# Expert stage: five row gathers ahead, units 0 and 1 interleaved, GpSimd drains at other places, a split norm vector and last product

## What is computed

```python
h2 = rmsnorm_2(x, norm2_g[l])
x = x + hier_moe(h2, ...)          # 32 experts of width 256, each token goes to 2 experts of one group
return rmsnorm_2(x, norm_f_g)

def expert_block(args):            # one block of rows, one expert
    xb, e = args
    return (jax.nn.silu(xb @ w_gate[e]) * (xb @ w_up[e])) @ w_down[e]
```

## Time and profile before

| | us |
|---|---|
| median of 3 runs | 1306.07 |
| the profiled execution, its time | 1303.1 |
| its span | 1301.1 |
| expert stage in the span | about 1056 to 1301 |
| TensorE busy | 1255.3 (96%) |
| VectorE / ScalarE / GpSimd busy | 640.0 / 522.9 / 568.9 |

### The profile page before, as it was taken

The page is one execution under the profiler, slowest core; times in us unless marked ns, Lnnn a source line. Parts: engine busy times, 40 slices in busy tenths (PEclk is TensorE's granted clock), DMA queues, the critical chain, the costliest instruction groups (busy, mean ns, idle before and its releaser), DMA issues.

```text
span 1301.1 us, 18979 instructions
## 1 busy us (share of the span) xinstructions
PE 1255.3 (96%) x6642; PEld 960.5 (74%) x6642; DVE 640.0 (49%) x1248; ACT 522.9 (40%) x884; POOL 568.9 (44%) x715
## 2 busy tenths in 40 slices
PE   7999999999999999999999999999999989998896
PEld 6767777787888888888888788777888865554462
DVE  4868768725542422222225765757243276342443
ACT  5657544435444324133144534145322300543444
POOL 4633323334655655555545664424644212341321
PEclk9999999999999999999999999999999999998899
DMA  6422222112334333333333333322427999999996
GB/s 219 109 65 55 67 58 65 50 49 81 98 96 113 115 97 97 115 97 113 97 98 97 97 96 83 82 49 70 126 81 265 359 331 386 417 417 416 417 417 246
DMA packets 223104, 208.38 MB, mean 160 GB/s; under 512 B 36034, under 2 KB 197556, under 8 KB 218804
## 3 DMA queue, kind: packets, MB, share of 16 engines
q1 hardware_dynamic: 209728, 191.87, 44.7%
q0 software_dynamic: 9504, 13.66, 2.8%
q10 hardware_dynamic: 3796, 1.86, 0.5%
HBM read 209.43 MB, written 20.45 MB: 177 GB/s over the span
## 4 chain that ended last, share of the span: by engine, by line
issue 40%; POOL 31%; PE 19%; DMA 4%; DVE 3%; SPq 2%; POOLq 1%; ACT 0%; DVEq 0%; ACTq 0%
POOL wlo L670 31%; PE bank L2408 4%; PE bank L2036 3%; PE bank L2038 3%; PE bank L2037 3%; PE bank L2425 3%; SPq L543 1%; DMA gu<-in_w_exp_up 1%; DMA xe<-part_rows,tabi 1%; PE side L2066 1%; DMA part_rows<-xe,tabi 1%; DMA xe<-x_rows,tabi 1%; PE side L2038 1%; PE side L2037 1%; PE side L2036 1%
## 5 line engine op out<-in xcount | busy, mean ns | idle before, releaser
L670 POOL TENSOR_TENSOR wlo<-raw,whi 128x256 fp32r<-128x256 f32 x644 | 497.6, 804 | 525.9 <-ACT whi L838 525.7
L2037 PE MATMUL bank<-actB_lo,whi 128*128 128x512 f32 x608 | 236.7, 389 | 0.0
L838 ACT ACTIVATE whi<-raw 128x1024 fp32r<-128x1024 f32 x161 | 169.0, 1051 | 152.6 <-PE bank L2038 125.0
L2036 PE MATMUL bank<-actB_hi,whi 128*128 128x512 f32 x576 | 227.8, 395 | 0.5 <-POOL wlo L670 0.5
L2038 PE MATMUL bank<-actB_hi,wlo 128*128 128x512 f32 x576 | 224.4, 390 | 0.0
L2036 PE MATMUL bank<-actA_hi,whi 128*128 128x512 f32 x400 | 157.0, 392 | 1.7 <-DVE actA_lo L1269 1.6
L2038 PE MATMUL bank<-actA_hi,wlo 128*128 128x512 f32 x400 | 155.7, 389 | 0.0
L2037 PE MATMUL bank<-actA_lo,whi 128*128 128x512 f32 x400 | 155.7, 389 | 0.0
L2408 PE MATMUL bank<-gu,xeT 128*64 128x256 f32 x1088 | 128.4, 386 | 8.5 <-issue 5.9
L2037 PEld LDWEIGHTS bank<-actB_lo,whi 128*128 128x128 f32 x608 | 114.2, 188 | 24.0 <-issue 1.0
L2036 PEld LDWEIGHTS bank<-actB_hi,whi 128*128 128x128 f32 x576 | 108.2, 188 | 25.9 <-issue 2.3
(11 more groups left out here) (448 smaller groups left out, 1703.3 us busy)
## 6 DMA issues: line engine op xcount, KB each, us to landing
gu<-in_w_exp_gate SPq DMA_DIRECT2D x64, 512.0 KB, 15.4
gu<-in_w_exp_up SPq DMA_DIRECT2D x64, 512.0 KB, 16.3
dn<-in_w_exp_down SPq DMA_DIRECT2D x30, 1024.0 KB, 17.8
raw<-in_w_in SPq DMA_DIRECT2D x57, 512.0 KB, 3.8
raw<-in_w_up SPq DMA_DIRECT2D x32, 512.0 KB, 3.9
raw<-in_w_down SPq DMA_DIRECT2D x32, 512.0 KB, 3.7
raw<-in_w_out SPq DMA_DIRECT2D x16, 512.0 KB, 3.8
raw<-in_w_in SPq DMA_DIRECT2D x16, 256.0 KB, 3.2
```

The costliest lines, as they stand in the source:

```text
L670: ins = nc.gpsimd.tensor_tensor(wlo[:, slot, at], raw[:, slot, at], whi[:, slot, at].bitcast(F32), ALU.subtract)
L838: a(whi[:, c % RING, :], raw[:, c % RING, :], ACT.Copy).then_inc(hi_made, 1)
L2036: mm(b[:, :], w_hi, hi[:, k, :], start=first, stop=False)
L2037: mm(b[:, :], w_hi, lo[:, k, :], start=False, stop=False)
```

## The change

- **Five gathers at once.** `buffer_of` now gives units 4 and 5 the buffers 5 and 4. Buffer 5 (`xe_far`) lies where `gfin` was, so POOL issues the gather of unit 4 with the first four. The waits for the scatters of units 0 and 1 ahead of gathers 4 and 5 are gone, and so is the wait for `over_ready` ahead of gather 6. Gather 5 waits for `over_listed`.
- **Norm vector in two pieces.** `gfin[0]` is loaded where `gfin` was. `gfin[1]` is loaded by SP after downs 8 and 9, behind a new wait for `over_ready`, because its place is used by a temporary until then. `finish` makes its product in two halves.
- **Loads of unit 4.** SP starts the quarters of unit 4 before it waits for the downs of unit 0.
- **Order of units 0 and 1 on TensorE.** Gates and ups of unit 0, rows of 1, gates and ups of unit 1, turn hidden 0, rows of 2, downs of 0, then iteration 1. The overflow table comes after the downs of unit 1. VectorE copies the rows of unit 1 ahead of `hidden(0)`, makes `hidden(1)` ahead of `y_of(0)`, and runs `list_overflow` after `y_of(1)`.
- **Drains.** The one ahead of scatter 13 is gone. There is now one ahead of `scattered(q)` and `parts_of_unit(q + 1)` for q = 7 and q = 8.
- **Last product shared.** In `finish_last` VectorE multiplies both halves by the gains while the norm is being worked out. Then VectorE scales the first half and ScalarE the second.
- The overflow loop counts its steps with two semaphores instead of five. It isn't entered with these inputs.

```diff
-    return q if q < X_FIRST else (0, 1, 4, 5, 2, 3)[(q - X_FIRST) % X_BUFS]
+    return q if q < X_FIRST else (5, 4, 0, 1, 2, 3)[(q - X_FIRST) % X_BUFS]
...
-            sp.dma_start(gfin[:, :], A["norm_f_g_2"].partition_broadcast(P)).then_inc(S("small_in"), 16)
+            sp.dma_start(gfin[0][:, :], A["norm_f_g_2"][0:L].partition_broadcast(P)).then_inc(S("small_in"), 16)
...
             for q in range(PIECED_E.start, EXTRA_AT + 1):
+                if q in PIECED_E:
+                    gate_up_in_quarters(q)
                 for n in places_of(q):
                     if n >= D_BUFS:
                         sp.wait_ge(S("down_done"), unit_of(n - D_BUFS) + 1)
                         down(n)
+                if q == PIECED_E.stop - 1:
+                    sp.wait_ge(S("over_ready"), 1)
+                    sp.dma_start(gfin[1][:, :], A["norm_f_g_2"][L:].partition_broadcast(P)).then_inc(S("small_in"), 16)
                 if q in PIECED_E:
-                    gate_up_in_quarters(q)
                     continue
...
-            for q in range(X_FIRST):
-                gather(q, tabi[:, 1, q:q + 1], S(f"gathered{q}"))
+            for q in range(X_FIRST + 1):
+                gather(buffer_of(q), tabi[:, 1, q:q + 1], S(f"gathered{q}"))
...
-                if q in (LAST_E - 3, LAST_E - 1):
+                if q == LAST_E - 1:
                     pool.drain()
                 pool.wait_ge(S("y_made"), q + 1)
                 scatter(buffer_of(q), tabi[:, 0, q:q + 1], S(f"scattered{q % 2}"))
                 n = q + X_FIRST
-                if n < UNITS_E:
-                    if q < 2:
-                        scattered(q)
-                    if q == 2:
+                if X_FIRST < n < UNITS_E:
+                    if q == 1:
                         pool.wait_ge(S("over_listed"), 1)
-                        pool.wait_ge(S("over_ready"), 1)
...
                 if q + 1 in MIXED_E:
+                    pool.drain()
                     scattered(q)
                     parts_of_unit(q + 1)
...
+            act.wait_ge(S("last_norm_made"), 1)
+            second = x_in(buffer_of(LAST_E))[:, L:]
+            a(second, second, ACT.Copy, scale=gw[:, 13, LAST_E % NT:LAST_E % NT + 1]).then_inc(S("last_squared"), 1)
...
+            def finish_last():
+
+                one_ = slice(LAST_E % NT, LAST_E % NT + 1)
+                first, second = (x_in(buffer_of(LAST_E))[:, n * L:(n + 1) * L] for n in range(2))
+                for n, x in enumerate((first, second)):
+                    dve.wait_ge(S("last_squared"), n + 1)
+                    chain(v.tensor_tensor(x, x, gfin[n][:, :], ALU.mult))
+                dve.wait_ge(S("guess_made"), guesses[0] + 1)
+                chain(v.tensor_tensor(gw[:, 12, one_], gw[:, 10, one_], gw[:, 11, one_], ALU.add))
+                refine(gw[:, 12, one_], gw[:, 13, one_], D, gw[:, 14, one_], gw[:, 15, one_], made=S("last_norm_made"))
+                chain(v.tensor_scalar(first, first, gw[:, 13, one_], None, ALU.mult), S("rows_finished"))
...
-            for q in range(LAST_E):
-                hidden(q % 2, slotv[:, 0, q:q + 1], q + 1)
-                if q == 0:
-                    rows_turned(1, 2)
-                    late_columns()
-                    overflow_columns()
-                    y_of(0)
-                    rows_turned(0, 3)
-                    place_overflow()
-                    continue
+            rows_turned(1, 2)
+            hidden(0, slotv[:, 0, 0:1], 1)
+            late_columns()
+            overflow_columns()
+            hidden(1, slotv[:, 0, 1:2], 2)
+            rows_turned(0, 3)
+            y_of(0)
+            place_overflow()
...
+            gate_up_of(0)
+            turn_rows_of(1)
+            first_gates_of(1, 0)
+            first_gates_of(1, 1)
+            gate_up_of(1)
+            turn_hidden(0, 1)
+            turn_rows_of(2)
+            down_of(0)
```

More of the change, by code:

```diff
@@ L364, in gated_blocks @@
         dn = [place(f"dn{n}", [P, 2, D], dn_at[n]) for n in range(D_BUFS)]
-        xe, _ = lay(b_at, ("xe", [P, X_BUFS, D]))
+        xe, gfin_at = lay(b_at, ("xe", [P, X_BUFS - 1, D]))
         hid, row_at, after4, after8, end3 = lay(s_at + 7 * half_buf, ("hid", [P, 2, DE]), ("row_at", [P, 2 * NT]),
@@ L379, in gated_blocks, with x_in @@
                                        ("over_at", [P, 3], I32), ("spare_rows", [P, 1], I32))
-        below = place("below", [1, OVER, NE], b_at + words([P, X_FIRST + 1, D]))
+        below = place("below", [1, OVER, NE], gfin_at)
         slotv = place("slotv", [P, 2, COLS], -(-tab_end // 64) * 64)
-        gfin = place("gfin", [P, D], base + 4 * CONST_COLS["cos"][0])
+        xe_far = place("xe_far", [P, D], base + 4 * CONST_COLS["cos"][0])
+        gfin = (place("gfin0", [P, L], base + 4 * CONST_COLS["before"][0]), place("gfin1", [P, L], gfin_at))
+        def x_in(n):
+            return xe[:, n, :] if n < X_BUFS - 1 else xe_far[:, :]
         lg, gw, vals, pos, pos_q, over_v, _ = lay(
@@ L1786, in finish @@
                     dve.wait_ge(S(f"scattered{q % 2}"), 16 * (q // 2 + 1))
-                chain(v.scalar_tensor_tensor(xe[:, buffer_of(q), :], xe[:, buffer_of(q), :], gw[:, 13, one_], gfin[:, :],
-                                             ALU.mult, ALU.mult), S("rows_finished"))
+                for n in range(2):
+                    x = x_in(buffer_of(q))[:, n * L:(n + 1) * L]
+                    ins = v.scalar_tensor_tensor(x, x, gw[:, 13, one_], gfin[n][:, :], ALU.mult, ALU.mult)
+                chain(ins, S("rows_finished"))
+            def finish_last():
[8 more added lines that the diff above has]
+                chain(v.tensor_scalar(first, first, gw[:, 13, one_], None, ALU.mult), S("rows_finished"))
             every_expert = const("iota")[:, 0:NE]
@@ L1927, in _ @@
             over = None
-            for q in range(LAST_E):
-                hidden(q % 2, slotv[:, 0, q:q + 1], q + 1)
-                if q == 0:
-                    rows_turned(1, 2)
-                    late_columns()
-                    overflow_columns()
-                    y_of(0)
-                    rows_turned(0, 3)
-                    place_overflow()
-                    continue
-                if q == 1:
-                    list_overflow()
+            rows_turned(1, 2)
[6 more added lines that the diff above has]
+            place_overflow()
+            for q in range(1, LAST_E):
+                if q > 1:
+                    hidden(q % 2, slotv[:, 0, q:q + 1], q + 1)
                 if q + 2 < UNITS_E:
@@ L1942, in _ @@
                 y_of(q)
-                if q == FINISH_FROM:
-                    dve.wait_ge(S("small_in"), 16 * (N_SMALL + 1))
+                if q == 1:
+                    list_overflow()
+                if q == FINISH_FROM + 1:
+                    dve.wait_ge(S("small_in"), 16 * (N_SMALL + 2))
                 if q > FINISH_FROM:
@@ L1986, in overflow @@
+                dve.wait_ge(S("over_dve_step"), i * 6 + (-1))
                 v.scalar_tensor_tensor(gw[:, 13, 1:2], gw[:, 15, 1:2], 1.5, gw[:, 13, 1:2], ALU.add, ALU.mult)\
-                    .then_inc(S("over_finished"), 1)
-                dve.wait_ge(S("over_finished"), i * 5)
+                    .then_inc(S("over_dve_step"), 1)
+                dve.wait_ge(S("over_dve_step"), i * 6)
                 dve.wait_ge(S("over_scattered"), i * 32 + (-16))
-                v.scalar_tensor_tensor(xe[:, OVER_X, :], xe[:, OVER_X, :], gw[:, 13, 1:2], gfin[:, :], ALU.mult, ALU.mult)\
-                    .then_inc(S("over_rows_done"), 1)
+                for n in range(2):
+                    x = x_in(OVER_X)[:, n * L:(n + 1) * L]
+                    ins = v.scalar_tensor_tensor(x, x, gw[:, 13, 1:2], gfin[n][:, :], ALU.mult, ALU.mult)
@@ L2005, in _ @@
                                        ALU.mult, ALU.add).then_inc(S("last_y_made"), 1)
-            finish(LAST_E)
+            finish_last()
         @block.tensor
@@ L2467, in _ @@
             turn_rows_of(0)
-            for q in range(LAST_E):
-                gate_up_of(q)
-                if q == 0:
-                    turn_rows_of(1)
-                elif q + 2 < UNITS_E:
+            gate_up_of(0)
[6 more added lines that the diff above has]
+            down_of(0)
+            for q in range(1, LAST_E):
+                if q > 1:
+                    gate_up_of(q)
+                if q + 2 < UNITS_E:
                     turn_rows_of(q + 2)
+                first_gates_of(q + 1, 0)
+                turn_hidden(q % 2, q + 1)
+                first_gates_of(q + 1, 1)
+                down_of(q)
                 if q == 1:
```

70 lines of the change are left out of this document (33 added, 37 removed).

## The result

The changed kernel takes 1321.78 us, the median of four runs (1317.32 to 1324.91), against 1305.51 for the kernel before (four runs): 1.0126, interval 1.0093 to 1.0158. It is slower both times. The forecast was 1310.5 with a range up to 1317.0. The sign was right, the size was less than half of what either measurement shows. The first lies above the range, the second inside it. The two profiled executions lie close together (spans of 1315.5 and 1314.3 us, against 1301.1 before), so the explanation goes by them. Why the medians of the two measurements differ by 6 us isn't shown.

A forecast was written before the change was run, and what follows sets the result against it. The stream of weights and TensorE were taken to run nearly level into the end. Drains +4.8, covering the stream's +1.4, and last product -0.4 gave +4.4 on 1306.07: 1310.5 us, range 1303.8 to 1317.0.

The forecast's parts named there:

- the +1.4 of the stream: Weights' queue dry before over_ready, so loads from unit 5 on run 1.4 us later; covered at the end by the drains' +4.8.
- TensorE in units 0 and 1: Reversed order starts unit 2 1.3 us earlier; with gathers 4 and 5 on time TensorE leads by 3.3 us until unit 8.
- The stream: Weight loads: gap at 1073 fills, engines dry 1088.0 to 1091.8, restart about 1095.0; 1.4 us later, ends 0 and +3.
- The first drain: Ahead of the gather for unit 8: store of unit 6 lands by 1176.7, gather goes at 1176.8, against 1177.13 before.
- The lead is used up (-0.3): At the gather for unit 8: issue at 1176.8 instead of 1177.13, though TensorE's lead moved the store ahead to 1164.3.
- The second drain: Ahead of the gather for unit 9: waits for a store, gather 5.6 us later, end +4.8 after 0.8 us of slack.
- the fetch: Instruction fetch at 1256 to 1257, ahead of scatter 13, taken to explain the 3.1 us after the last POOL landing.
- the open part: The 3.1 us between the last POOL landing and scatter 13; if the drain's own, it counts at both new drains.
- The drain that was removed: Ahead of scatter 13: removal lets that scatter go earlier, but the chain doesn't pass through it; no gain counted.
- The last product: At the kernel's end: 512 columns on each of two engines instead of 1024 on one, gaining 0.35 us (0 to 0.6).
- The rival of the costlier drains: Each new drain costs 3 us more, gather for unit 9 11.8 late, end +10.6: 1316.7; chance 0.16.
- the second rival: Drains hidden, the wait for over_ready decides and the stream sets the end: +1.0, 1307.1; chance 0.28.

The follow-up runs named there:

- e2_old_drains: Changed kernel with the drains back ahead of scatters 13 and 15, the new wait for over_ready kept: 1306.61 us, 1.0014 of the kernel before.
- e3_both: Changed kernel with gfin[1] and its wait moved behind unit 5's loads and the drains where they were before: 1302.70 us, 0.9982 of the kernel before.
- e8_after_again: The changed kernel unaltered, measured a second time: 1315.91 us, 1.0088 of the kernel before.
- e1_gfin_late: Changed kernel with the wait for over_ready and the gfin[1] load moved behind unit 5's loads, new drains kept: 1312.21 us, 1.0049 of the kernel before.
- e15_both_drains: The kernel of e1_gfin_late run again, on one chip with e12_neither: 1310.10 us, 1.0049 of the kernel before.
- e7_one_drain: Changed kernel with gfin[1] and its wait behind unit 5's loads, and only the drain ahead of scatter 15: 1302.51 us, 0.9986 of the kernel before.
- e12_neither: The kernel of e7_one_drain run again, on one chip with e15_both_drains: 1302.60 us, 0.9989 of the kernel before.
- e9: e7_one_drain plus the drain ahead of the gather of partial sums for unit 8 alone: 1.0012 of the kernel before.
- e10: e7_one_drain plus the drain ahead of the gather of partial sums for unit 9 alone: 1.0052 of the kernel before.
- e11: e7_one_drain with gates and ups of units 6 to 8 loaded ahead of their downs on SP: 1303.28 us, 0.9996 of the kernel before.

## Why the prediction was right or wrong

The forecast failed at the stream of weights, and by less at the drains. The sum put the new wait for over_ready at nothing ("This covers the +1.4 of the stream"). The runs show 3.9 us for it with the old drains (e2_old_drains against e3_both) and about 5 on top of the new ones (1.0088 in e8_after_again against 1.0049 in e1_gfin_late and e15_both_drains). The drains cost 7.5 to 9.5 us and not 4.8. Term by term:

- **TensorE in units 0 and 1: right.** Unit 2 starts 1.29 us earlier from the start of unit 0 (1.3 forecast), unit 4 3.19 (3.3 forecast). "TensorE then leads by 3.3 us until unit 8" was wrong in its last three words. The lead shrinks or ends at the gates of unit 7, even in kernels without the early wait: TensorE stood 1.38 us for them in e3_both, 3.14 in e1_gfin_late, 3.80 in e7_one_drain. I had checked the stream's reserve at its end only. Before, the last of these gates landed at 1144.1 (issued at 1125.0, 19.1 us to landing) and TensorE began with them at 1144.73, so a lead had nowhere to go.
- **The stream: the mis-sized term.** 1.4 us was forecast, with +3 as the upper end. The queue's bytes say 4.8. The parts beyond the forecast: SP went on at 1094.52 and not at 1093.1 (1.4, of which 1.04 is the late unit 0); 252 instead of 415 GB/s over the 4 us behind the gap (1.6). The rest of 0.4 stays within the reading. The slow 4 us are `gfin[1]`: the sum had 1.3 + 0.6 = 1.9 us from its issue until it had moved, and it took 5.1. Between other loads the 0.6 would have been near (e1_gfin_late), at the head of an empty queue it wasn't. The larger error was in the reading of where it counts. It was taken to matter at the end, covered by the drains, while TensorE met it at unit 7 and stood 6.03 us, after which the next gates took 1.97 instead of 1.08. The comparisons put it at 3.9 us with the old drains, and with the new drains unit 11 starts 1.9 to 6.7 us later by it (169.94 and, in e8_after_again, 172.21 us behind unit 0; without the wait 168.00 in e1_gfin_late and 165.52 in e15_both_drains, which are one kernel).
- **The first drain: wrong because of the step before.** "The lead is used up (-0.3)" put the store of unit 6 at 1164.3. It was issued at 1177.50 and, in e8_after_again, at 1175.52, where it landed 13.2 later (12.4 was my longest). There the gather for unit 8 went 6.9 us behind the landing of its scatter. That cost 1.4 us at the end in the median where the stream is in order.
- **The second drain: right in mechanism, near in size.** Its gather goes 5.1 us behind the landing of the scatter in e8_after_again, 5.6 forecast. As a lone first drain it is 7.8, since 2.3 us come on top of the landing. These I had put down to the fetch and left out at these places. TensorE stood 7.31 and 6.65 us ahead of unit 11 in the two profiles, and not 10, since the wait ahead of unit 10 had already come to 3.26 and 5.45. The third reading of the open part, that it belongs to the first drain only, I hadn't thought of.
- **The drain that was removed: right,** it was worth nothing (0.9982 and 0.9986).
- **The last product: half.** From the start of the last sum to the store it takes 5.04 us (1307.37 to 1312.41), before 5.21 (1292.86 to 1298.07): 0.17 gained, 0.35 forecast. The two halves took 0.49 and 0.72 us, and ScalarE is the later one:

```profile
1310.74 0.49 DVE L1814 TENSOR_SCALAR xe_far<-xe_far,gw 128x512 f32<-128x512 f32 x1
1310.80 0.72 ACT L1224 ACTIVATE xe_far<-xe_far,gw 128x512 f32<-128x512 f32 x1 [1.29 <-DVE gw L1247]
1312.41 0.98 POOL L712 DMA_INDIRECT out<-xe_far,tabi  x1 [6.18 <-ACT xe_far L1224]
```

- **The sum.** Forecast: nothing for the stream, +4.8 for the drains, -0.4 for the product. Measured: about +4 to +5 for the wait, +7.5 to +9.5 for the drains, -1.3 to -1.8 for all the rest. That is about 10 to 13, which holds the second measurement (+12.1) but not the first (+16.3). The rival of the costlier drains had 1316.7, near the second measurement's 1315.9, but by a sum that holds no part of the stream. The hidden drains of the second rival are refuted. The stores ahead of the two gathers landed after 8.5 to 13.5 us, with the weights' queue full. The rule of the Trainium skill that stands beside that rival ("DMA: Bandwidth & Descriptors", section "Anatomy of one DMA — SWDGE (gpsimd) path") gives about 3.2 us for such a store of 0.52 MB, an estimate from its 2.0 us and 436 GB/s. The trace comes near it only at the kernel's last store (2.6 us), and here the measurement decides. The range ended at 1317.0, since the drains' upper bound and the stream's were never taken together.

The version that beats the kernel before is e7_one_drain (and e3_both, e12_neither): the change with `gfin[1]` loaded behind unit 5 and no drain ahead of the gathers of partial sums, 0.2% faster in three comparisons (0.9982, 0.9986, 0.9989).

## What to carry to other kernels

Where TensorE and the stream of weights run level, compare them at every unit and not only at the end: a wait on the weights' queue costs what goes beyond its reserve at its tightest point, and a lead won upstream ends there. Read a drain as a wait for every transfer that the engine has started, unneeded stores and prefetches too, and keep it from standing ahead of a transfer on the path. A small load of short rows at the head of an empty queue holds up all that stands behind it, so start it behind loads that are already flowing. Undo suspects one by one and together on one chip, since slack and the clock can pay for one of them and not for both.

## What the runs showed of the hardware

- GpSimd's drain lasted to the landing of its last transfer and 0.9 to 1.0 us more (five readings), or 2.2 to 3.1 us more where it was the first of the program (eleven readings).
- `gfin[1]`, 128 rows of 2 KB, took 5.1 to 6.1 us from issue to landing at the head of the empty queue (three profiles), and the weights behind it waited: 252 GB/s over 4 us (153 in e2_old_drains), the DMA engines busy for 0.99 (0.86). With a load of weights first, behind a shorter gap, the queue moved 387 GB/s in the next 4 us.
- A wait of TensorE of 4.19 us was followed by some 6 us at 1.2 GHz and cost 3 us more than itself (e12_neither). One of 4.06 us cost 1.8 more (e2_old_drains: gates 1.59, downs 4.84), one of 1.43 us nothing. A wait of 1.55 us ahead of the downs of unit 15 was followed by the lower clock in some executions and not in others, also of one and the same kernel (e1_gfin_late and e15_both_drains, and the changed kernel's two profiles).
- In four profiles (the changed kernel's first, e9, e10 and e11) ScalarE started 0.85 to 0.95 us behind TensorE's last matmul of a unit in five or six of the 17 units, where the other profiles show 0.05. Three of these kernels were run again on other chips or at another time and didn't show it.
